# A mixture-of-experts block: the overflow rounds behind the main round, and two loads of work in front of the first expert rearranged

## The reference

```
logits = h @ w_router + b_router                 # 256 x 32
gates  = softmax over the best 4 of each token
for each expert e, over the tokens that chose it:
    gate, lin = split(h @ w_gate_up[e] + b_gate_up[e])
    gate, lin = min(gate, 7), clip(lin, -7, 7)
    y += gates[e] * ((gate * sigmoid(1.702 * gate) * (lin + 1)) @ w_down[e] + b_down[e])
x = x + g2 * y
```

## Time and profile before

| | us |
|---|---|
| runs | 1657.16, 1658.79, 1665.58; median 1658.79 |
| the profiled execution | 1655.59 |
| its span, first to last instruction | 1653.8 |
| busy in it: TensorE, VectorE, ScalarE | 1560.8, 555.9, 437.0 |

### The profile page before, as it was taken

One profiled execution on the slowest core, in us unless ns is written; L12 is line 12 of the kernel. 1 busy time (PEld: TensorE's weight loads), 2 busy tenths in 40 slices (PEclk: granted clock), 3 DMA queues, 4 the chain that ended last, 5 costly groups with the idle time before them and its releaser, 6 DMA issues.

```text
span 1653.8 us, 22441 instructions
## 1 busy us (share of the span) xinstructions
PE 1560.8 (94%) x9426; PEld 933.1 (56%) x9426; DVE 555.9 (34%) x1088; ACT 437.0 (26%) x885; POOL 7.2 (0%) x17
## 2 busy tenths in 40 slices
PE   4999888999999999999999999999899999989998
PEld 2797673443434434344333333333399988889986
DVE  3748541110111111111111111111245564467774
ACT  3435620110111011011101101101244563256553
POOL 0000000000000000000000000000000100000000
PEclk9999998999999999999999999999999999989999
DMA  9325675999999999999999999999944534434530
GB/s 392 146 102 239 276 262 238 432 427 425 431 431 432 430 432 432 431 432 430 432 431 431 431 431 432 432 432 431 426 164 160 186 112 169 159 136 165 204 128 26
DMA packets 27445, 526.56 MB, mean 318 GB/s; under 512 B 2931, under 2 KB 6003, under 8 KB 7492
## 3 DMA queue, kind: packets, MB, share of 16 engines
q1 hardware_dynamic: 24080, 519.58, 75.3%
q10 hardware_dynamic: 2772, 4.22, 0.9%
q0 software_dynamic: 512, 1.57, 0.4%
HBM read 524.28 MB, written 1.08 MB: 318 GB/s over the span
## 4 chain that ended last, share of the span: by engine, by line
PE 73%; DMA 21%; DVE 3%; ACT 1%; issue 1%; SPq 0%; ACTq 0%; DVEq 0%
PE ps L638 71%; DMA ring<-in_w_down 19%; DMA ring<-in_first 1%; PE ps L766 1%; DMA arena<-in_ctxT 1%; DMA arena<-in_b_gate_up 1%; DVE ring_r L1729 0%; PE ps L967 0%; PE ps L1141 0%; PE ps L960 0%; ACT arena L1545 0%; DVE hx_lo L1736 0%; DVE arena L1742 0%; DVE arena L2169 0%; DVE arena L2170 0%
## 5 line engine op out<-in xcount | busy, mean ns | idle before, releaser
L638 PE MATMUL ps<-ring,arena 128*64 128x512 f32 (+1 forms) x3840 | 706.1, 531 | 25.4 <-DMA ring<-in_w_down 16.5
L638 PEld LDWEIGHTS ps<-ring,arena 128*64 128x64 f32 (+1 forms) x3840 | 234.7, 131 | 442.4 <-issue 401.8
L638 PE MATMUL ps<-arena 128*128 128x128 f32 (+9 forms) x1732 | 306.3, 411 | 29.1 <-issue 11.6
L638 PEld LDWEIGHTS ps<-arena 128*128 128x128 f32 (+4 forms) x1732 | 178.5, 179 | 157.3 <-issue 137.2
L638 PE MATMUL ps<-arena_r,w_high 128*128 128x256 f32 x1360 | 247.8, 285 | 0.0
L1981 DVE TENSOR_SCALAR arena<-ps 128x512 f32<-128x512 f32 x32 | 22.1, 691 | 570.7 <-PE ps L638 570.7
L638 PEld LDWEIGHTS ps<-arena_r,w_high 128*128 128x128 f32 x1360 | 212.2, 192 | 2.9 <-issue 1.7
L638 PE MATMUL ps<-arena_r,ring_r 128*128 128x256 f32 x680 | 192.3, 283 | 0.0
L2036 DVE TENSOR_TENSOR ring_r<-ring,w_high 128x1024 fp32r<-128x1024 f32 x120 | 142.2, 1220 | 96.1 <-ACT w_high L1514 96.1
L1467 ACT ACTIVATE arena<-ps 128x256 f32<-128x256 f32 x32 | 12.3, 383 | 453.7 <-PE ps L960 453.7
L1514 ACT ACTIVATE w_high<-ring 128x1024 fp32r<-128x1024 f32 x120 | 121.3, 1054 | 34.6 <-PE ps L638 32.3
(11 more groups left out here) (216 smaller groups left out, 1044.3 us busy)
## 6 DMA issues: line engine op xcount, KB each, us to landing
ring<-in_w_gate_up SPq DMA_DIRECT2D x64, 4096.0 KB, 19.4
ring<-in_w_down SPq DMA_DIRECT2D x32, 4096.0 KB, 18.4
ring<-in_second SPq DMA_DIRECT2D x32, 2048.0 KB, 7.9
ring<-in_first SPq DMA_DIRECT2D x18, 2048.0 KB, 16.8
arena<-in_memory SPq DMA_DIRECT2D x4, 1024.0 KB, 11.6
ring<-in_second SPq DMA_DIRECT2D x2, 1024.0 KB, 4.8
arena<-in_xT SPq DMA_DIRECT2D x1, 1024.0 KB, 7.9
arena<-in_ctxT SPq DMA_DIRECT2D x1, 1024.0 KB, 10.8
```

The source lines that it names most:

```text
L638: return nc.tensor.matmul(out_, lhsT, rhs, start=start, stop=stop, **kw)
```

## The change

Three things change. First, the overflow rounds move behind the main round, on all four engines. They use the main round's semaphores, go on counting where it ended, and have a simpler body of their own: a loop over single experts without pipelining, once on each engine. TensorE and SP still read the count before the main round and keep it in a register; ACT and DVE read it behind the round. Second, `b_gu` is loaded right behind `b_down`, before ACT's eight bias loads, and TensorE waits for it only in front of expert 0's biases. Third, the first gather's second half goes to PSUM bank 3, so that it needn't wait until ACT has copied the first half out of bank 2.

```diff
@@ SP
-            with sp.If(count > SLOTS):
-                with sp.Fori(0, ROUNDS_MORE) as r:
-                    base = r * (UNITS_EXPERT * N_EXPERTS) + 1
-                    stream(more_units, base, more_full)
...
             sp.wait_ge(bias_mm, 1)
             sp.dma_start(final_row, io["rows"][:, 0, :]).then_inc(rows_in, 16)
-            stream(moe_units, 0, slot_full, True)
+            stream()
+            with sp.If(count > SLOTS):
+                with sp.Fori(1, ROUNDS_MORE + 1) as r:
+                    with sp.Fori(0, N_EXPERTS) as e:
+                        for q, src in ((0, w_gu[e, 0]), (1, w_gu[e, 1]), (2, w_dn[e])):
+                            sp.wait_ge(moe_units, (r * N_EXPERTS + e) * UNITS_EXPERT + (q - 2))
+                            pair_of(q, src, more_full)
+                sp.wait_ge(moe_units, (ROUNDS_MORE + 1) * N_EXPERTS * UNITS_EXPERT)
@@ PE
-            pe.wait_ge(bgu_in, 16)
...
+            def more_pe(r):
+
+                with pe.Fori(0, N_EXPERTS) as e:
+                    n = r * N_EXPERTS + e
+                    pe.wait_ge(s_ready, n + (2 - N_EXPERTS // 2))
+                    for half in range(2):
+                        gather(half, SLOTS)
+                        pe.wait_ge(x_ready, n * 2 + (1 + half - N_EXPERTS))
+                    pe.wait_ge(sel_ready, n + 2)
+                    add_expert_biases()
+                    for q in range(2):
+                        pe.wait_ge(more_full[PAIRS[q]], n * 16 + (16 - 16 * N_EXPERTS))
+                        gate_up(0, q, q)
+                    turn_hidden(n)
+                    turn_gates(n)
+                    pe.wait_ge(at_ready, n + 1)
+                    pe.wait_ge(sgt_ready, n + 2)
+                    pe.wait_ge(more_full[PAIRS[2]], n * 16 + (16 - 16 * N_EXPERTS))
+                    down(2, 0)
+                    down(2, 1)
+                    pe.wait_ge(y_ready, n + 2)
+                    for last in combine():
+                        pass
+                    last.then_inc(more_done, 1)
...
-                pe.wait_ge(S.s_ready, r * 17 + 1)
-                gather(0)
-                if S is MAIN:
-                    add_biases(0)
-                gathered(0, False)
-                gather(1)
-                if S is MAIN:
-                    add_biases(1)
+                pe.wait_ge(s_ready, 1)
+                gather(0, 2 * SLOTS)
+                gather(1, 2 * SLOTS, 3)
+                add_biases(0)
+                add_biases(1)
+                pe.wait_ge(bgu_in, 16)
+                biases(0)
                 gathered(0, True)
-                biases(0)
...
-            with if_more(pe):
-                for q in range(3):
-                    pe.wait_ge(slot_full[PAIRS[q]], 16 * (fills1(PAIRS[q]) + 1))
-                    pe.sem_inc(more_full[PAIRS[q]], 16)
-                pe.sem_inc(more_units, 1)
-                with pe.Fori(0, ROUNDS_MORE) as r:
-                    round_pe(MORE, r)
-                for q in range(3):
-                    pe.wait_ge(more_full[PAIRS[q]], 16 * (ROUNDS_MORE * N_EXPERTS + 1))
-            round_pe(MAIN, 0)
+            pe.wait_ge(most_set, 1)
+            count = pe.value_load(most_i[0:1, 0:1], min_val=0, max_val=T)
+            round_pe()
+            with pe.If(count > SLOTS):
+                with pe.Fori(1, ROUNDS_MORE + 1) as r:
+                    more_pe(r)
@@ ACT
             act.dma_start(b_dn[0:N_EXPERTS], io["b_down"][0]).then_inc(bdn_in, 16)
+            act.wait_ge(bgu_zero, 1)
+            act.dma_start(b_gu[0:N_EXPERTS], io["b_gate_up"][0]).then_inc(bgu_in, 16)
             act.wait_ge(bias_out, 16)
             bias_loads(act, 0, bias_in)
...
             load_table(ACT.Exp)
-            act.wait_ge(bgu_zero, 1)
-            act.dma_start(b_gu[0:N_EXPERTS], io["b_gate_up"][0]).then_inc(bgu_in, 16)
...
+            def more_act(r):
+
+                with act.Fori(0, N_EXPERTS) as e:
+                    n = r * N_EXPERTS + e
+                    for half in range(2):
+                        copy_gather(half, n * 2 + (1 + half - N_EXPERTS), SLOTS)
+                    sigmoid(n)
+                    copy_hidden(n)
+                    copy_gates(n)
...
                 for half in range(2):
-                    copy_gather(half, r * 32 + (half + 1))
+                    copy_gather(half, half + 1, 2 * SLOTS, 2 + half)
...
+            round_act()
             act.wait_ge(most_set, 1)
             with act.If(act.value_load(most_i[0:1, 0:1], min_val=0, max_val=T) > SLOTS):
-                with act.Fori(0, ROUNDS_MORE) as r:
-                    round_act(MORE, r)
-                    act.wait_ge(MORE.round_done, r + 1)
-            round_act(MAIN, 0)
-
+                with act.Fori(1, ROUNDS_MORE + 1) as r:
+                    more_act(r)
+                act.wait_ge(more_done, ROUNDS_MORE * N_EXPERTS)
@@ DVE
+            def more_dve(r):
+
+                V.tensor_scalar(rank[:], rank[:], -float(SLOTS), None, ALU.add).then_inc(shifted, 1)
+                with dve.Fori(0, N_EXPERTS) as e:
+                    n = r * N_EXPERTS + e
+                    dve.wait_ge(shifted, r)
+                    one_hot(e, 0).then_inc(s_ready, 1)
+                    selector(e)
+                    gated(e)
+                    dve.wait_ge(moe_units, n * UNITS_EXPERT + 2)
+                    hidden_act(n, n + 2)
+                    dve.wait_ge(moe_units, n * UNITS_EXPERT + 3)
+                    V.tensor_tensor(y_e, ps[:, 3, :], g2_rows, ALU.mult).then_inc(y_ready, 1)
...
+            round_dve(before_experts)
             dve.wait_ge(most_set, 1)
             with dve.If(dve.value_load(most_i[0:1, 0:1], min_val=0, max_val=T) > SLOTS):
-                with dve.Fori(0, ROUNDS_MORE) as r:
-                    round_dve(MORE, r, None)
-                V.tensor_scalar(rank[:], rank[:], float(ROUNDS_MORE * SLOTS), None, ALU.add).then_inc(MORE.shifted, 1)
-                dve.wait_ge(MORE.shifted, ROUNDS_MORE + 1)
-            round_dve(MAIN, 0, before_experts)
+                with dve.Fori(1, ROUNDS_MORE + 1) as r:
+                    more_dve(r)
+                dve.wait_ge(more_done, ROUNDS_MORE * N_EXPERTS)
```

More of the change, by code:

```diff
@@ L890, in memory_chunk @@
                 last.then_inc(kv_mm, 1)
[L892 to L901, removed]
-                    for t in range(TT):
[L904 to L919, removed]
@@ new lines, in wide, with gather @@
+            def wide(q, a):
+                return ring[:, PAIRS[q]:PAIRS[q] + 2, :].rearrange("p a n -> p (a n)").rearrange("p (a n) -> p a n", a=a)
+            def gather(half, width, bank=2):
+                for c in range(4):
+                    for t in range(TT):
+                        last = mm(ps[:, bank, P * c:P * c + width], x1_tm[:, t, P * (4 * half + c):P * (4 * half + c) + P],
+                                  s_hot[:, t].rearrange("p a b -> p (a b)")[:, 0:width], t == 0, t == TT - 1)
+                last.then_inc(gather_mm, 1)
@@ L920, in biases, with gate_up @@
+            def gate_up(j, q, second_half):
+                w = wide(q, 4)
+                for kk in range(4):
+                    k = 4 * second_half + kk
                     for n in range(2):
@@ L945, in down @@
[L945 to L952, removed]
-                    if part:
-                        last.then_inc(S.units, 1)
@@ new lines, in turn_gates, with turn_hidden @@
+            def turn_gates(e):
+                pe.wait_ge(sg_ready, e + 1)
+                for t in range(TT):
+                    last = nc.tensor.transpose(ps[:, 3, P * t:P * t + P], sg_hot[:, t, :], ident)
+                last.then_inc(sgt_mm, 1)
+            def turn_hidden(e):
+                pe.wait_ge(a_ready, e + 1)
+                for b in range(4):
+                    last = nc.tensor.transpose(ps[:, 2, P * b:P * b + P], a_e[:, P * b:P * b + P], ident)
+                last.then_inc(at_mm, 1)
@@ new lines, in copy_gather, with sigmoid @@
+            def copy_gather(half, n, width, bank=2):
+                act.wait_ge(gather_mm, n)
+                for c in range(4):
+                    k = 4 * half + c
+                    last = A(xg[:, k, 0:width], ps[:, bank, P * c:P * c + width], ACT.Identity,
+                             bias=modcol[:, 24 + k, 0:1], scale=scale2[:, k:k + 1])
+                last.then_inc(x_ready, 1)
+            def sigmoid(e):
+                act.wait_ge(g_ready, e + 1)
+                A(sig_e, g_e, ACT.Sigmoid, scale=SWIGLU_ALPHA).then_inc(sig_ready, 1)
```

271 lines of the change are left out of this document (125 added, 146 removed).

## The result

The changed kernel takes 1650.22 us (median of five runs, 1646.74 to 1650.84), the kernel before 1660.86 beside it (1657.16 to 1665.58): a ratio of 0.9933, 95% interval 0.9911 to 0.9955, so 11.1 us less (7.5 to 14.8). A second timing, of the same kernel beside two others, gave 0.9941 (0.9923 to 0.9958). The profiled execution took 1646.74 us, with a span of 1644.9, against 1655.59 and 1653.8 before: 8.9 us less. These two executions both lie under their medians, by 3.5 and 5.3 us. The forecast was 1648.9 us and -9.9.

A forecast was written before the change was run, and what follows sets the result against it. The prediction took the DMA queue to bound the expert stage, its end following the first load. -10.4 us in front plus 0.5 at the tail gave -9.9: 1648.9 us against the median 1658.79; range 1646 to 1656.5 (0.86).

The forecast's parts named there:

- Expert biases earlier: Router's chain: bias load moves from 236.99 to near 204 us, shifting ACT's eight loads 0.65 us; costs nothing, 0.65 uncovered.
- The jump goes: In front of the first gather: TensorE keeps only the read, so the gather starts at 245.4 instead of 254.34 us.
- its fetch waits behind the memory loads: At TensorE's old jump: 6.07 us read as a code fetch at the target, waiting behind 3 MB of memory loads.
- 9.5 us from the gather to the gate-up: First gather to expert 0's gate-up: 10.96 us becomes 9.5; 1.45 from the clock, two banks worth next to nothing.
- the prediction's bound: First gather to expert 0's gate-up: if the clock falls nonetheless, the 1.45 us stay.
- First pair load 10.4 us earlier: Expert stage's start: expert 0's gate-up at 254.9 instead of 265.30 us, first pair load near 262.
- The stage's end moves with the first issue, microsecond for microsecond: Expert stage: the queue doesn't run dry after its first issue, so the load's 10.4 us gain reaches the stage's end.
- the queue alone as the bound: Expert stage, 272.5 to 1176 us: DMA queue busy all the time at 430 GB/s, 391 MB taking 909 us.
- TensorE's 24 us of idle time: Expert stage: TensorE busy 879 of 903.5 us, cited as some slack for the not-passed-on rival (chance 0.07).
- Tail +0.5: Behind the last expert: DVE's read has no cover, 1.18 - 0.70 = 0.48 us lost; bounds 0 and 1.1.
- Rival, a fetch at the end: Behind the last expert: jump fetches code; sum -9.4 if TensorE's, -7.4 ACT's, -3.8 DVE's; part given back, chance 0.12.

The follow-up runs named there:

- experiments 1 and 2: 1: changed kernel with old bias load, old wait and one bank, ratio 0.9953; 2: kernel before with TensorE's overflow body cut to one instruction, issue gap 1.39 us.
- experiment 3: Kernel before with SP's three memory loads issued behind the wait for the bias products; issue gap 5.06 us instead of 7.25, span 1653.2 us.
- experiment 6: Kernel before with two banks alone: first gather to gate-up 10.76 us (10.96 before); changed kernel with one bank: 11.0 us (9.16 with two).
- stream_late: Changed kernel with SP's first pair load of the expert stage held until the second gate-up unit is done; span 1657.0 us.
- one_bank: Changed kernel with the first gather back in one bank and its bias products between the halves; span 1649.8 us.
- bias_late: Changed kernel with the expert-bias load back in the router's chain, its wait still in front of expert 0's biases; span 1647.1 us.
- experiment 9: Changed kernel with count reads in front, four down-bias products behind expert 0's second unit, row load behind first `in_second`; ratio 0.9934 to kernel before.
- experiments 9 and 10: 10: like 9, but two down-bias products in front of the first gather and two behind expert 0's second unit; ratio 0.9907 to kernel before.
- after_again: The changed kernel once more, unaltered, timed as a yardstick; ratio 0.9941 to the kernel before.

## Why the prediction was right

By its own steps:

- *Expert biases earlier: nothing, hidden.* Issued at 203.75, out of the chain; ACT's next work started at 210.79 (210.93 before). The eight bias loads begin 1.45 us later, not 0.65, which is hidden too: they end at 209.28.
- *The jump goes: the first gather 1.2 us behind `most_i`.* 1.0 measured; TensorE's read ended before the one-hots did. That the jump over the long body costs, not the read, is shown by experiments 1 and 2. That its fetch waits behind the memory loads is true for 2.2 of the 6.1 us at most (experiment 3); the prediction put no share on it, but read it as the cause.
- *9.5 us from the gather to the gate-up, 1.45 of them the clock's gain, the banks next to nothing.* 9.16 at full clock; the banks 0.25 to 0.45 (experiment 6). That the clock was full was in part luck: of the eight executions in which only the routing holds the first gather, five have 1.00 there and three (stream_late, one_bank, bias_late) 0.52 to 0.56, though TensorE stood idle for no longer in front of it (1.7 us) than in the changed kernel. There the 1.45 us stay away, as the prediction's bound had it.
- *First pair load 10.4 us earlier.* 9.5 in the trace; counted from `most_i`, 11.0 (28.38 to 17.41). The sum was sized well by its parts, and the routing was 1.5 us late in that execution.
- *The stage's end moves with the first issue, microsecond for microsecond.* 901.1 to 900.7 us, and 6.9 for 7.0 when delayed. As a general statement it is wrong: 3.6 us more in front brought nothing (experiment 9). The units of TensorE that free the later slots count as well (experiments 9 and 10). The prediction named the queue alone as the bound, and read TensorE's 24 us of idle time over the stage as a whole; but in the kernel before TensorE is busy for all of 300 to 500 us, with the queue's share at 0.99 to 1.01, and 20 of the 24 us of idle time lie behind 700. It held for the change because the units moved with the first issue: expert 1's gate-up, too, starts 10.9 us nearer to `most_i` than before (38.3 and 27.4 us), the stage's end 11.4.
- *Tail +0.5.* +0.66, on VectorE as said.
- *Rival, a fetch at the end.* It most likely took place on TensorE, under 6.20 us of cover, and cost nothing. VectorE goes on after 0.83 us of "issue" and ScalarE with no delay, so neither missed. The prediction called TensorE's fetch likely because 300 instructions are more than one page of 256. The rule that it goes by, of the Trainium skill (Runtime: NRT & Kernel Launch, Instruction fetch mechanics), has a window of two pages, so this count alone made a fetch possible, not likely.

Sum from the trace, in order: `most_i` +1.5, gap -9.15, products -1.8, stage -0.4, tail +0.7, the first 32 products of the second block +0.7 (6.35 us against 5.62), the rest -0.4 = -8.85; the spans differ by 8.9. The 0.7 of those 32 products is no price of the change: in after_again they take 5.23 us behind the same idle time. So the hit on the number has some chance in it: counted from `most_i` the stage's end moved by 11.4 us, more than the 10.4 forecast, and a late routing and a slow second block took part of it back in the profiled execution.

## What to carry to other kernels

A branch body that never runs can still cost: the jump over an unrolled round took 6 us here, on the critical path of the one engine with the long body. Put such a branch where its engine waits anyway, make its body short, and read its condition ahead of time on every engine. And before pulling loads forward, look which engine frees the slots of the later ones: 3.6 us on the first load alone were worth nothing; 2.6 us on TensorE's third unit, with the first load 2.9 us earlier, were worth 2.3.

## What was not expected of the hardware

- The jump over the long body costs 3.9 us even with an idle DMA queue, most of the 6.1. With the queue full at the tail (share 1.00 from 1187 to 1193.2 us) the page was moved before 1190 all the same.
- The same router products take 3.8, 5.4 or 6.4 us, and the changed kernel's gather stretch 9.16 or 10.6, by the granted clock under them. So a stretch of equal code differs by 1 to 2.6 us from one profile to the next, up to a quarter of what this change is worth; the stage's end counted from `most_i` agrees to 0.1 us in three executions where the clock does.
